# One attention layer, three gate groups: a new order of the work on VectorE, ScalarE, GpSimd and TensorE

## What is computed

```python
def second_block(x, w_in, b_forget, w_branch, w_out, ...):
    proj = jnp.einsum('bsd,dc->bsc', x, w_in[layer])
    (qa, ka, va, qi, ki, wi, qf, kf, vf, fg, qs, ks_, vs, gates) = jnp.split(proj, split_at, axis=-1)
    o_a = _dsa_attention(...)          # softmax over the 64 best keys of an index score
    o_b = _forgetting_attention(...)   # softmax of q.k + c_q - c_k
    o_c = _stick_breaking_attention(...)
    # log_beta = log_sigmoid(z); log_one_minus = log_sigmoid(-z) below the diagonal
    # a = exp(log_beta + sum of log_one_minus over later keys)
    branches = jnp.stack([o_a, o_b, o_c], axis=0)
    up = jnp.einsum('ibsw,iwd->bsid', branches, w_branch[layer])
    g = jax.nn.sigmoid(gates.reshape(b, s, N_BRANCHES, D_MODEL))
    merged = jnp.sum(up * g, axis=2)
    y = jnp.einsum('bsd,de->bse', merged, w_out[layer])
    x = _layer_norm(DEEPNORM_ALPHA * x + y, ln1_g[layer], ln1_b[layer])
```

## Time and profile before

| | before |
|---|---|
| time, median of three runs | 1469.51 us (1469.36 to 1471.5) |
| the profiled execution | 1470.54 us |
| its span, first to last instruction | 1468.7 us |
| PE, DVE, ACT, POOL busy, share of the span | 99%, 86%, 63%, 13% |
| waits of PE between 1090 and 1265 us, sum of its five rows | 4.4 us |
| granted TensorE clock, mean | 0.999 |

### The profile page before, as it was taken

The page is one execution under the profiler, slowest core; times in us unless marked ns, Lnnn a source line. Parts: engine busy times, 40 slices in busy tenths (PEclk is TensorE's granted clock), DMA queues, the critical chain, the costliest instruction groups (busy, mean ns, idle before and its releaser), DMA issues.

```text
span 1468.7 us, 19076 instructions
## 1 busy us (share of the span) xinstructions
PE 1454.5 (99%) x7580; PEld 1234.1 (84%) x7580; DVE 1267.7 (86%) x1289; ACT 926.6 (63%) x981; POOL 185.2 (13%) x184
## 2 busy tenths in 40 slices
PE   9999999999999999999999999999999999999997
PEld 8888888888888888888888888888998877899996
DVE  7899877789998899889966789987797789889998
ACT  6666666566666666665634666656647888466665
POOL 0000110200002000026130200002002300020001
PEclk9999999999999999999999999999999999999999
DMA  9898554589859689556644689944653674587762
GB/s 370 264 325 263 186 201 172 196 291 276 270 170 332 210 280 305 161 191 234 187 170 172 261 249 280 308 155 183 230 164 123 201 258 151 193 328 245 228 223 65
DMA packets 50775, 333.17 MB, mean 227 GB/s; under 512 B 6032, under 2 KB 6480, under 8 KB 13056
## 3 DMA queue, kind: packets, MB, share of 16 engines
q1 hardware_dynamic: 38592, 270.35, 47.6%
q0 software_dynamic: 10288, 57.87, 18.7%
q10 hardware_dynamic: 1808, 3.74, 0.7%
HBM read 282.60 MB, written 1.05 MB: 193 GB/s over the span
## 4 chain that ended last, share of the span: by engine, by line
PE 85%; DVE 9%; DMA 4%; issue 1%; ACT 1%; POOL 0%; POOLq 0%; SPq 0%; DVEq 0%; ACTq 0%
PE psum L2738 11%; PE psum L2742 11%; PE psum L2741 11%; PE psum L2971 7%; PE psum L2975 7%; PE psum L2972 7%; PE psum L2847 4%; DVE weights_lo L1642 4%; PE psum L2874 3%; PE psum L2851 2%; PE psum L2770 2%; PE psum L2881 2%; PE psum L2783 2%; PE psum L2776 2%; PE psum L3576 2%; PE psum L3572 2%
## 5 line engine op out<-in xcount | busy, mean ns | idle before, releaser
L1642 DVE TENSOR_TENSOR weights_lo<-weights_raw,weights_hi 128x2048 fp32r<-128x2048 f32 (+1 forms) x158 | 350.9, 2223 | 79.6 <-ACT weights_hi L863 79.0
L863 ACT ACTIVATE weights_hi<-weights_raw 128x2048 fp32r<-128x2048 f32 (+1 forms) x171 | 304.1, 1782 | 132.6 <-PE psum L2742 68.8
L1642 DVE TENSOR_TENSOR weights_lo<-weights_raw_more,weights_hi 128x2048 fp32r<-128x2048 f32 (+1 forms) x74 | 145.4, 1968 | 5.1 <-ACT weights_hi L863 5.1
L863 ACT ACTIVATE weights_hi<-weights_raw_more 128x2048 fp32r<-128x2048 f32 (+1 forms) x84 | 132.2, 1586 | 5.9 <-DVE weights_raw_more L2591 3.6
L2738 PE MATMUL psum<-weights_hi,hidden_hi 128*128 128x512 f32 x300 | 119.1, 397 | 1.2 <-DVE weights_lo L1642 1.2
L2741 PE MATMUL psum<-weights_lo,hidden_hi 128*128 128x512 f32 x300 | 117.3, 391 | 0.0
L2742 PE MATMUL psum<-weights_hi,hidden_lo 128*128 128x512 f32 x300 | 117.1, 390 | 0.0
L2738 PE MATMUL psum<-weights_hi,operand 128*128 128x512 f32 x256 | 100.9, 394 | 0.7 <-issue 0.7
L2741 PE MATMUL psum<-weights_lo,operand 128*128 128x512 f32 x256 | 100.1, 391 | 0.0
L2742 PE MATMUL psum<-weights_hi,operand 128*128 128x512 f32 x224 | 87.3, 390 | 0.0
L2874 PE MATMUL psum<-operand,weights_hi 128*128 128x512 f32 x320 | 80.5, 393 | 0.7 <-issue 0.7
(11 more groups left out here) (558 smaller groups left out, 3742.1 us busy)
## 6 DMA issues: line engine op xcount, KB each, us to landing
weights_raw<-in_weights SPq DMA_DIRECT2D x141, 1024.0 KB, 5.3
weights_raw_more<-in_weights SPq DMA_DIRECT2D x76, 1024.0 KB, 9.3
normalised<-in_weights SPq DMA_DIRECT2D x23, 1024.0 KB, 4.9
ln_rows<-in_weights SPq DMA_DIRECT2D x14, 1024.0 KB, 8.1
weights_raw<-weights_raw POOLq DMA_DIRECT2D x13, 1024.0 KB, 11.1
weights_raw_more<-ln_rows POOLq DMA_DIRECT2D x8, 1024.0 KB, 6.9
ln_rows<-in_ln_rows POOLq DMA_DIRECT2D x16, 512.0 KB, 5.3
ln_rows<-normalised POOLq DMA_DIRECT2D x5, 1024.0 KB, 15.9
```

Of the source, the lines that this page charges most:

```text
L863: nc.scalar.activation(hi[:, rest], whole[:, rest], ACT.Copy).then_inc(hi_split, 1)
L1642: nc.vector.tensor_tensor(lo_of(n), raw_of(n), hi_of(n).bitcast(F32), ALU.subtract).then_inc(lo_split, 1)
```

## The change

No operation is added or removed: the calls in the lists of POOL, ACT and DVE, and a few places in PE's `between`, change their order. The order of SP's loads is the same. Of the diff, the pieces that the prediction speaks of (POOL; ACT; DVE around group 1 and group 2; PE):

```diff
             add_gate_t4(0)
+            add_gate_t1(1)
             scale_weights(1, 0)
-            add_gate_t1(1)
             scale_weights(1, 1)
             scale_weights(1, 2)
...
             group_hi(0, 6)
+            softmax_exp(1, 0)
             gate_copy(0, 2)
-            softmax_exp(1, 0)
             unit_hi(9, 0)
...
             half_copy(9, 0, a_k[:, 0])
             group_hi(1, 1)
-            group_hi(1, 2)
             half_copy(9, 1, a_k[:, 0])
             pt_copy(1, range(0, 4))
+            group_hi(1, 2)
...
+            stick_small(0)
             up_hi_split(0, 0)
-            stick_small(0)
             stick_ln(0)
...
             logits(1, 2)
+            inverse_sums(1, 1)
             group_lo(1, 0)
-            inverse_sums(1, 1)
             inverse_sums(1, 2)
             half_sum(9, 0, a_k[:, 0])
             group_lo(1, 1)
+            half_sum(9, 1, a_k[:, 0])
             gate_t2(1)
             group_lo(1, 2)
             gate_t3(1)
-            half_sum(9, 1, a_k[:, 0])
...
             stick_beta(1)
-            stick_sum(0)
             stick_logs(1)
             group_lo(2, 3)
+            group_lo(2, 4)
             stick_lo(1)
-            group_lo(2, 4)
+            stick_sum(0)
             group_lo(2, 5)
             stick_sum(1)
...
-            gate_group(0, between={2: lambda: turn_p(0, range(4, 8)), 3: lambda: (softmax_values(0), forget_logits(0)), 4: lambda: forget_logits(1), 6: lambda: forget_logits(2)})
+            gate_group(0, between={0: lambda: turn_p(0, range(0, 4)), 2: lambda: turn_p(0, range(4, 8)), 3: lambda: (softmax_values(0), forget_logits(0)), 5: lambda: forget_logits(1), 6: lambda: forget_logits(2)})
...
-            gate_group(2, between={0: lambda: stick_later(0), 4: lambda: stick_later(1), 6: lambda: stick_values()})
+            gate_group(2, between={0: lambda: stick_later(0), 5: lambda: stick_later(1), 6: lambda: stick_values()})
```

More of the change, by code:

```diff
@@ L1419, in _ @@
             unit_hi(7, 1)
+            unit_hi(8, 0)
+            unit_copy(6, as_pair(a_k[:, 1]))
             softmax_exp(0, 0)
-            unit_hi(8, 0)
             softmax_exp(0, 1)
             unit_hi(8, 1)
-            unit_copy(6, as_pair(a_k[:, 1]))
+            group_hi(0, 0)
             unit_copy(7, a_v[:, 1])
-            group_hi(0, 0)
             softmax_exp(0, 2)
@@ L1432, in _ @@
             group_hi(0, 2)
+            gate_copy(0, 0)
             group_hi(0, 3)
+            gate_copy(0, 1)
+            pt_copy(0, range(4, 8))
             group_hi(0, 4)
-            pt_copy(0, range(4, 8))
-            gate_copy(0, 0)
             group_hi(0, 5)
-            gate_copy(0, 1)
             out_hi(0)
             group_hi(0, 6)
+            softmax_exp(1, 0)
             gate_copy(0, 2)
-            softmax_exp(1, 0)
             unit_hi(9, 0)
@@ L1458, in _ @@
             group_hi(1, 3)
+            gate_copy(1, 1)
             group_hi(1, 4)
             out_hi(1)
-            gate_copy(1, 1)
             group_hi(1, 5)
             gate_first(1)
+            gate_copy(1, 2)
             group_hi(1, 6)
-            gate_copy(1, 2)
             unit_hi(10, 0)
             stick_abs(0)
+            gate_second(1)
             unit_hi(10, 1)
-            gate_second(1)
             gate_last(1)
+            stick_small(0)
             up_hi_split(0, 0)
-            stick_small(0)
             stick_ln(0)
@@ L1482, in _ @@
             group_hi(2, 2)
+            group_hi(2, 3)
             gate_copy(2, 0)
+            group_hi(2, 4)
             gate_copy(2, 1)
-            group_hi(2, 3)
-            group_hi(2, 4)
             stick_hi(1)
             group_hi(2, 5)
-            stick_exp(0)
             gate_copy(2, 2)
             group_hi(2, 6)
+            stick_exp(0)
             stick_exp(1)
@@ L2460, in _ @@
             logits(0, 0)
-            logits(0, 1)
             unit_lo(7, 1)
             unit_lo(8, 0)
+            logits(0, 1)
+            inverse_sums(0, 0)
             logits(0, 2)
-            inverse_sums(0, 0)
             unit_lo(8, 1)
+            group_lo(0, 0)
             inverse_sums(0, 1)
-            group_lo(0, 0)
             inverse_sums(0, 2)
@@ L2472, in _ @@
             gate_t2(0)
+            half_sum(8, 1, a_q[:, 0], HEAD_DIM ** -0.5)
             group_lo(0, 2)
-            half_sum(8, 1, a_q[:, 0], HEAD_DIM ** -0.5)
+            group_lo(0, 3)
             gate_t3(0)
-            group_lo(0, 3)
             group_lo(0, 4)
             gate_sum(0)
+            group_lo(0, 5)
+            logits(1, 0)
             out_lo(0)
-            logits(1, 0)
-            group_lo(0, 5)
             group_lo(0, 6)
             gate_less(0, 0)
+            inverse_sums(1, 0)
             logits(1, 1)
             gate_less(0, 1)
-            inverse_sums(1, 0)
             unit_lo(9, 0)
@@ L2497, in _ @@
             gate_t3(1)
-            half_sum(9, 1, a_k[:, 0])
             group_lo(1, 3)
             group_lo(1, 4)
+            out_lo(1)
             gate_sum(1)
-            out_lo(1)
             group_lo(1, 5)
             stick_mask(0)
+            gate_less(1, 0)
             group_lo(1, 6)
-            gate_less(1, 0)
             gate_less(1, 1)
@@ L2536, in _ @@
             up_lo_split(1, 1)
-            up_lo_split(0, 2)
             gate_product(0, 1)
             out_lo(2)
+            up_lo_split(0, 2)
             up_lo_split(1, 2)
+            gate_add(0, 1)
             gate_product(1, 1)
+            gate_add(1, 1)
+            gate_product(0, 2)
+            gate_add(0, 2)
             split_lo(N_SEC_OUT)
[L2543 to L2546, removed]
             turn_lo("mrg", x_hi, x_lo, range(2), swap=2)
+            split_lo(N_SEC_OUT + 1)
             gate_product(1, 2)
             gate_add(1, 2)
-            split_lo(N_SEC_OUT + 1)
             split_lo(N_SEC_OUT + 2)
@@ L3536, in stick_values @@
                 values(2, a_p)
-            unit(6, features_unit, between={0: lambda: index_logits(0)})
-            unit(7, tokens_unit, between={0: lambda: index_logits(1), 3: lambda: index_logits(2)})
-            both_pairs(8, between={7: lambda: turn_p(0, range(0, 4))})
-            gate_group(0, between={2: lambda: turn_p(0, range(4, 8)), 3: lambda: (softmax_values(0), forget_logits(0)), 4: lambda: forget_logits(1), 6: lambda: forget_logits(2)})
+            unit(6, features_unit, between={6: lambda: index_logits(0)})
+            unit(7, tokens_unit, between={0: lambda: index_logits(1), 2: lambda: index_logits(2)})
+            both_pairs(8)
+            gate_group(0, between={0: lambda: turn_p(0, range(0, 4)), 2: lambda: turn_p(0, range(4, 8)), 3: lambda: (softmax_values(0), forget_logits(0)), 5: lambda: forget_logits(1), 6: lambda: forget_logits(2)})
             both_pairs(9)
```

6 lines of the change are left out of this document (3 added, 3 removed).

## The result

The changed kernel takes 1478.18 us (median of six runs, 1476.46 to 1478.73), the kernel before 1470.5 us (six runs beside them, 1469.36 to 1472.17). The ratio is 1.0045, with a 95% interval of 1.0035 to 1.0056: slower by 5 to 8 us. The profiled execution took 1476.46 us, with a span of 1474.7 us and a mean granted clock of 0.995, where it was 0.999.

What follows compares the result with a forecast made beforehand. The prediction took TensorE, busy 99% of the span, as the bound, so only its waits could move; 5.1 - 0.9 + 0.1 = +4.3 us on the profiled 1470.54 gave 1474.8, as median 1473.8, range 1469.0 to 1476.5.

Steps and rivals of the forecast that it cites:

- the sum: Whole kernel: 5.1 us wait in group 1, less 0.9 in group 2, plus 0.1 in group 0: +4.3 us.
- The wait at `turn_p(1)`: Group 1: PE waits 5.1 us for POOL's scaled weights, held up by VectorE instructions with two SBUF inputs.
- the price of part 1: Group 1: group_lo(1, 0) meets POOL's part 1 of the scaling, so part 2 would end 0.65 us late, the floor.
- early t1: Group 1: t1, moved ahead of scale_weights(1, 0) on POOL, is issued at 1146.9 and lands at 1156.4 with 9.5 us.
- the term of the clock: Group 1: the sum added nothing for a clock fall in PE's wait; the fall stood only as a rival.
- the rival's price: Clock falls during the 5.1 us wait: 2 us more, 1475.8; full wait with or without the fall had 0.62.
- Group 2: Stick branch moves gain 0; the chain starts 0.9 us earlier behind t1 of group 2, all of it gained.
- Group 0 and the end: gate_copy(0, 2) behind the exponentials costs 0.1 us; other moves there and behind group 2 meet no PE wait.
- From the profile to the median: Profiled execution before, 1470.54 us, stood 1.03 us above the median 1469.51, so 1474.8 became 1473.8.
- 1474.8 less or more the 1.92 us of one subtraction: Likeliest case by itself, around the profiled time, given as 1472.5 to 1476.5.

Runs made afterwards that it cites:

- one-input experiment: Changed kernel with group_lo(1, 0) and group_lo(1, 1) each a sum over the raw tile, one SBUF input instead of two: 1470.51 us, ratio 0.9996.
- the one with t1 put back: Changed kernel with add_gate_t1(1) put back behind scale_weights(1, 0): 1477.97 us, ratio 1.0046.
- the two edits: Kernel before with only add_gate_t1(1) ahead of scale_weights(1, 0) and inverse_sums(1, 1) ahead of group_lo(1, 0): 1481.42 us; run again for a long execution's profile, 1480.42 us.
- the kernel with the stick branch's order alone: Kernel before with the stick branch's new order in group 2 alone, on VectorE, PE and ScalarE: 1471.43 us, ratio 1.0002.
- the one with both edits undone: Changed kernel with inverse_sums(1, 1) back behind group_lo(1, 0) and add_gate_t1(1) back behind scale_weights(1, 0): 1473.01 us, ratio 1.001.
- the repaired one: Changed kernel with inverse_sums(1, 1) back behind group_lo(1, 0) and half_sum(9, 1) moved ahead of group_lo(1, 1): 1470.07 us, ratio 0.9995.
- the reciprocal back: Changed kernel with inverse_sums(1, 1) put back behind group_lo(1, 0): 1473.71 us, ratio 1.0021.
- `half_sum` moved alone: Changed kernel with half_sum(9, 1) moved ahead of group_lo(1, 1), inverse_sums(1, 1) still ahead of group_lo(1, 0): 1470.99 us, ratio 0.9997.

## Why the prediction was right or wrong

The direction, the place and the mechanism were right. Sizes were wrong, and the time came out above the range: 1478.18 against 1473.8 and an upper end of 1476.5. In the profiles the sum said +4.3 us, and 5.9 were measured (1470.54 to 1476.46).

- **The wait at `turn_p(1)`**: 5.1 us predicted, 4.8 measured. The steps stand: t1 issued at 1145.16 (1146.9 predicted) landed after 9.1 us (9.5 taken), `group_lo(1, 1)` began at 1159.60 (1159.85), `gate_t2(1)` at 1162.53 (1162.8), POOL ended at 1165.05 (1165.7). The one-input experiment shows the cause, and 0.65 us as the price of part 1 is confirmed with 0.6 us. That early t1 comes from the move on POOL's queue was only half true: the earlier `inverse_sums(1, 0)` gives it as well.
- **The step that failed** is the term of the clock, which the sum puts at nothing: the fall during the wait stands only among the rivals. The prediction read from the end of the program that the clock had fallen 4.3 us after PE's stop, had a wait of 5.1 us, and still summed without the fall. In all three profiles with a wait of 4.8 us or more (the changed kernel, the one with t1 put back, the long one of the two edits) the clock fell: 2.3 us after PE's stop in the first and the third, and 4.8 us after it, as PE came back, in the second. It cost 2.0 us in the changed kernel; the rival's price, 2 us, was right.
- **Group 2** is the second term that was wrong: a gain of 0.9 us was predicted, a loss of 0.6 measured. PE was 6.51 us behind the kernel before at the values of branch 1 (1175.45 against 1168.94) and 7.13 us behind it past group 2 (L3474 at 1269.99, before at 1262.86). The three waits there were 3.0 us and are 1.9 us, but the clock's fall behind the wait for `stick_sum(0)`, which no step had, took 1.6 us of PE's time. Nor is the gain shown to come from the moves: 0.7 us of it is the wait at L2971, behind the transfer of t1 of group 2, and that wait is gone as well in the kernel with the stick branch's order alone and in both profiles of the two edits, which move nothing between that transfer and this wait. The transfer took 12.3 us before, 11.7, 10.6 and 11.2 us in these three and 10.1 us in the changed kernel. Over the runs the moves in group 2 are worth nothing.
- **Group 0 and the end**: 0.1 us predicted. PE was done with what stands ahead of `turn_p(1)` 0.34 us earlier than before (1159.23 + 1.11 = 1160.34 against 1159.57 + 1.11 = 1160.68), having been 0.5 us ahead since 93 us, so some 0.2 us went between, over group 0 and also over units 6 to 8, whose moves the section on the change doesn't name. Nothing that counts.
- **Luck**: the clock and group 2 together put 3.5 us on top of the sum, and yet the profile is only 1.7 us above it, since 1.65 us fell away outside the attention layer: 0.5 ahead of it, and 1.15 behind it, as the last matmul is 5.98 us later than before (1467.15 against 1461.17) and not 7.13. PE of the kernel before waited 0.5 us for weights at 93 us and 0.4 us at 1450 us in its profile, that of the changed one at neither place. That the rival's 1475.8, with the 1.03 us added back 1476.8, lies so near the 1476.46 of the profile is owed to the same.
- **From the profile to the median** the prediction subtracted 1.03 us, from three runs. With six, the kernel before stands at 1470.5, where its profile is, so there was nothing to subtract; and the changed kernel's profile is the shortest of its six runs, 1.72 us under their median. These 2.75 us are the larger part of the 4.4 us that were missed; the sum was short by 1.7 us. Why the six differ by up to 2.3 us stays open.
- **Two slips** on which nothing hangs: by its own rows part 1 alone ends at 1154.68 + 1.84 = 1156.52, not at 1157.1; and 1474.8 less or more the 1.92 us of one subtraction is 1472.9 to 1476.7, not 1472.5 to 1476.5.

## What to carry to other kernels

Where GpSimd does elementwise work that TensorE is about to need, look at what VectorE starts beside it: here instructions with two inputs in SBUF held it up, and ones with an input in PSUM or with one input didn't. An earlier transfer or an earlier start isn't free if it moves such an instruction into that stretch; here the execution whose transfer landed 5.5 us earlier was 9.5 us longer, while with both `half_sum` ahead of `group_lo(1, 1)` and the reciprocal put back the early transfer cost nothing. And a wait of TensorE of a few microseconds is to be priced with the clock's fall behind it, which here added 2.0 us to a wait of 4.8. A sum that comes near the measured time is to be checked term by term: here two of its terms were wrong by 3.5 us together, and half of that was hidden by waits that fell away elsewhere.

## What the hardware showed beyond that

A head of the scaling can be held by more than one instruction. In the long execution of the two edits the longest head took 4.52 us, where one alone takes 0.35 to 0.46 (ns, least, median, most):

```profile
L792 POOL TENSOR_SCALAR att_p<-att_p,att_sum x32: 369/476/4517, 1104.3 to 1169.3; 128x256 f32<-128x256 f32 x16, 128x128 f32<-128x128 f32 x16
```

The Trainium skill, page "SBUF — State Buffer", section "Who interferes with whom", has the later instruction wait for the end of the other one. The trace agrees that it waits, and here it waited through two: these 4.52 us are about two VectorE instructions of 2.28 us, so when VectorE's next one stood ready, GpSimd's lost a second time. The four VectorE instructions beside it lost at most 0.16 us each (2.44 instead of 2.28).

The same wait of 1.7 us at L3415 was followed by a fall of the clock in the profiles of four kernels (the changed one, the one with both edits undone, the repaired one and the one with group 2's order alone) and not in those of four others (the reciprocal back, t1 back, the one-input kernel, `half_sum` moved alone). A wait of 2.0 us at L3376 was followed by none in either of two profiles, one of 2.6 us at L2738 by a fall in the only one. What decides it stays open.
